# The RWKV stage of a five-block fp32 network: queues rearranged, and the squared keys for the norms in two fp32r parts

## The reference, cut to what matters

```python
def rwkv7_time_mix(x, mu, w_rkv, ...):
    xx = shift(x) - x                      # previous token minus this one
    xr, xw, xk, xv, xa, xg = (x + xx * mu[i] for i in range(6))
    r, k, v = xr @ w_r, xk @ w_k, xv @ w_v
    w = decay(tanh(xw @ w1) @ w2);  a = sigmoid(a0 + (xa @ a1) @ a2)
    g = sigmoid(xg @ g1) @ g2
    kk = normalise(k * k_k)                # per head of 64: divide by the root of the sum of squares
    k = k * (1 + (a - 1) * k_a)
    # per head, token by token: S = S*w + (S @ -kk) (kk*a)^T + v k^T ; y = S @ r
    return (group_norm(y) + bonus) * g @ w_o
```

## Time and profile before

| | us |
|---|---|
| median of 3 runs | 2152.41 (2149.99 to 2152.99) |
| the profiled execution | 2152.05 |
| its span in the trace | 2150.2 |
| busy in it: PE / DVE / ACT / POOL | 2005.9 / 871.6 / 928.4 / 923.5 |
| RWKV projections, first LoRA matmul to last V matmul | about 752.9 to 962.2 |

### The profile page before, as it was taken

The page is one execution under the profiler, slowest core; times in us unless marked ns, Lnnn a source line. Parts: engine busy times, 40 slices in busy tenths (PEclk is TensorE's granted clock), DMA queues, the critical chain, the costliest instruction groups (busy, mean ns, idle before and its releaser), DMA issues.

```text
span 2150.2 us, 32846 instructions
## 1 busy us (share of the span) xinstructions
PE 2005.9 (93%) x13218; PEld 1586.3 (74%) x13218; DVE 871.6 (41%) x1793; ACT 928.4 (43%) x1721; POOL 923.5 (43%) x641
## 2 busy tenths in 40 slices
PE   6999899999997899897888999999989999999998
PEld 5888566787765675676675888887877678888786
DVE  2103566310037494865654433331043733333301
ACT  3342677343256566532333544432153744344312
POOL 3332577244356434520127344445424634444542
PEclk9999999999998999996899999999999999999999
DMA  4323100233210222222102233333213022333322
GB/s 146 89 73 99 40 1 2 69 91 107 80 40 30 79 69 71 69 79 58 30 20 98 60 97 95 92 98 118 95 54 97 2 94 84 97 98 98 118 89 79
DMA packets 222376, 161.53 MB, mean 75 GB/s; under 512 B 28602, under 2 KB 205314, under 8 KB 222226
## 3 DMA queue, kind: packets, MB, share of 16 engines
q1 hardware_dynamic: 220034, 152.36, 23.9%
q0 software_dynamic: 2192, 7.07, 1.1%
HBM read 154.16 MB, written 5.24 MB: 74 GB/s over the span
## 4 chain that ended last, share of the span: by engine, by line
PE 78%; DVE 11%; ACT 3%; issue 3%; POOL 3%; DMA 1%; POOLq 1%; DVEq 0%; PEld 0%; PEldq 0%; SPq 0%; ACTq 0%
PE ps L389 15%; PE ps L351 13%; PE ps L353 13%; PE ps L362 13%; PE ps L399 7%; PE ps L1443 2%; PE ps L1456 2%; PE ps L1432 2%; DVE ps L970 1%; DVE buffer L3200 1%; POOL weights_lo L292 1%; DVE buffer L978 1%; DVE buffer L3202 1%; PE ps L2233 1%; PE ps L2255 1%
## 5 line engine op out<-in xcount | busy, mean ns | idle before, releaser
L292 POOL TENSOR_TENSOR weights_lo<-buffer,weights_hi 128x1024 fp32r<-128x1024 f32 (+1 forms) x266 | 659.4, 2481 | 901.1 <-ACT weights_hi L281 900.8
L281 ACT ACTIVATE weights_hi<-buffer 128x1024 fp32r<-128x1024 f32 (+1 forms) x266 | 277.9, 1048 | 298.9 <-PE ps L399 274.1
L351 PE MATMUL ps<-u_hi,weights_hi 128*128 128x512 f32 (+1 forms) x752 | 280.1, 380 | 5.6 <-DVE u_lo L706 3.0
L353 PE MATMUL ps<-u_lo,weights_hi 128*128 128x512 f32 (+1 forms) x736 | 279.6, 384 | 0.0
L2031 ACT ACTIVATE buffer<-ps,buffer 128x512 f32<-128x512 f32 x88 | 68.5, 778 | 282.9 <-PE ps L362 282.9
L2061 DVE SCALAR_TENSOR_TENSOR buffer<-ps,buffer,buffer 128x511 f32<-128x511 f32 x88 | 66.0, 750 | 294.2 <-ACT buffer L2031 294.2
L362 PE MATMUL ps<-u_hi,weights_lo 128*128 128x512 f32 (+1 forms) x752 | 176.6, 377 | 0.0
L351 PEld LDWEIGHTS ps<-u_hi,weights_hi 128*128 128x128 f32 x752 | 141.5, 190 | 33.1 <-issue 5.6
L353 PEld LDWEIGHTS ps<-u_lo,weights_hi 128*128 128x128 f32 x736 | 138.3, 188 | 30.0
L362 PEld LDWEIGHTS ps<-u_hi,weights_lo 128*128 128x128 f32 x752 | 136.5, 190 | 26.8 <-POOL weights_lo L292 0.2
L389 PE MATMUL ps<-weights_hi,act_hi 128*128 128x512 f32 x352 | 111.3, 397 | 0.5 <-issue 0.5
(11 more groups left out here) (431 smaller groups left out, 4117.4 us busy)
## 6 DMA issues: line engine op xcount, KB each, us to landing
buffer<-in_w_up SPq DMA_DIRECT2D x88, 512.0 KB, 3.8
buffer<-in_w_down SPq DMA_DIRECT2D x44, 512.0 KB, 3.3
buffer<-in_diff_w_in SPq DMA_DIRECT2D x32, 512.0 KB, 4.0
buffer<-in_nsa_w_in SPq DMA_DIRECT2D x28, 512.0 KB, 3.8
buffer<-in_w_rkv SPq DMA_DIRECT2D x24, 512.0 KB, 3.8
buffer<-in_nsa_w_out SPq DMA_DIRECT2D x8, 512.0 KB, 3.6
buffer<-in_diff_w_out SPq DMA_DIRECT2D x8, 512.0 KB, 3.7
buffer<-in_w_o_rwkv SPq DMA_DIRECT2D x8, 512.0 KB, 3.4
```

Source lines behind the costliest of these rows:

```text
L281: self.nc.scalar.activation(self.part_hi[:, part % self.PARTS, 0:n], self.raw[:, ld % self.RAW, 0:n], ACT.Copy).then_inc(self.hi_ready, 1)
L292: self.nc.gpsimd.tensor_tensor(self.part_lo[:, part % self.PARTS, 0:n], self.raw[:, ld % self.RAW, 0:n], self.part_hi[:, part % self.PARTS ...
L351: nc.tensor.matmul(out, hi[:, k, :], rhs[0][:, k, tokens], start=(k == 0), stop=False)
L353: nc.tensor.matmul(out, hi[:, k, :], rhs[1][:, k, tokens], start=False, stop=False)
```

## The change

1. **Norms.** The plain fp32 product of the squared keys becomes two fp32r products. DVE makes the raw square (`scalar_tensor_tensor` of K, k_k squared, K), ACT copies its high part, DVE subtracts for the low part, each in a single buffer. ACT's own square is gone. `squares(0)` and `squares(1)` both stand behind K2, and `squares(j-1)` behind Kj.
2. **Mix scratch** of the key and gate mixes moves from SBUF to PSUM banks 5 and 6. The mixes of V and R are made inside DVE's key loop, four for each j from 4 on.
3. **Second LoRA product** is interleaved with the gate products, so ACT's 16 sigmoids run beside them.
4. **Receptance loop.** `sums` 0 to 3 come before it, 4 to 7 in its first four rounds. `blocks` 0 to 3 stand behind R4 to R7; their upper halves are copied by DVE, in its own round.
5. **Values and core.** `blocks` 4 to 7 move from the core's list into the first V half. The blocks are stored piece by piece, the first four before the first slot of the second V half is fetched. The second inversion starts with the first item of the core's list.
6. **Transition.** The first half of the LoRA product comes after all four turns of x, with DVE's and ACT's items reordered.

The core of the diff (the loop with the mixes is DVE's, the one with `high` and `take` is ACT's):

```diff
         for j in range(2, KD):
             project_features(env, pe, self.k[j][0], m.mixes[self.K], self.k[j][1])
-            squares(j - 2)
+            if j == 2:
+                squares(0)
+            squares(j - 1)
...
+        for j in range(KD):
+            pair = (2 * j % KD, 2 * j % KD + 1)
+            for n in (self.G,) if j < 4 else (self.MIXED_V, self.MIXED_R):
+                for k in pair:
+                    mix(n, k)
+            if j < 4:
+                for k in pair:
+                    low(self.G, k)
+            if j:
+                square_low(j - 1)
+            square(j)
...
             high(n, k)
             high(n, k + 1)
+            if j:
+                square(j - 1)
             env.split_hi(act, ahead[j + 2])
             take(entry, m.k[:, j, :], ACT.Copy)
-            act.wait_ge(env.proj_taken, entry[1] + 1)
-            square(j)
...
         def blocks(n):
-            if n:
-                pe.wait_ge(self.core.blocks_taken, n)
-            else:
-                pe.wait_ge(self.shrink_taken, NT + 1)
+            pe.wait_ge(self.shrink_taken, NT if n < NT else KD)
+            if n:
+                pe.wait_ge(self.core.blocks_act, n)
+                pe.wait_ge(self.core.blocks_dve, n)
...
-            if k >= 5:
-                blocks(k - 5)
+            if k >= NT:
+                blocks(k - NT)
...
-            if k + 3 < KD:
-                sums(k + 3)
+            if k < NT:
+                sums(k + NT)
+            if k > NT:
+                take_blocks(k - 1 - NT)
             dve.wait_ge(env.proj_taken, g + 1)
             v.tensor_tensor(m.r[:, k, :], m.r[:, k, :], shrink, ALU.mult).then_inc(self.shrink_taken, 1)
...
-        self.order = [(name, 0) for name in first] + [("dg", n) for n in range(NT, 2 * NT)] + [(name, 1) for name in first]
+        self.order = [(name, n) for n in range(2) for name in first]
```

More of the change, by code:

```diff
@@ L2435, in __init__ @@
         self.blkX = env.take(BLK, BLK, at=slot(6))
-        self.diag = [env.take(32, BLK, at=slot(6)), second]
+        later = self.v[:, :, T:T + 256].rearrange("p n (u t) -> p n u t", t=BLK)
+        first = env.take(32, BLK, at=slot(6))
+        self.diag = [first[:, 8 * n:8 * n + 8, :] for n in range(NT)] + [later[:, n] for n in range(NT)]
         self.rk = [env.take(2, T, at=env.post_g_at), env.take(2, T, at=env.pair_at)]
@@ L2599, in tensor, with second @@
+            squares(j - 1)
         hid_hi, hid_lo = [h[:, 0, :] for h in m.hid]
         hi, lo = env.parts(self.second)
+        def second(k):
+            if k >= 2:
+                pe.wait_ge(env.proj_taken, self.second_group(k - 2, 1) + 1)
+            cols = slice(k * P, (k + 1) * P)
+            for w, x, first, last in ((hi, hid_hi, True, False), (hi, hid_lo, False, False), (lo, hid_hi, False, True)):
+                for which, rows in enumerate((slice(0, 64), slice(64, P))):
+                    done = mm(env.ps[:, 2 * (k % 2) + which, :], w[rows, 0, cols], x[rows, :], start=first, stop=last)
+                    if last:
+                        done.then_inc(env.proj_ready, 1)
@@ new lines, in gate_highs, with gate_lows @@
+        def gate_highs(n):
+            w, (x_hi, x_lo) = env.parts(self.g1[n])[0], m.mixes[self.G]
+            out = env.ps[0:w.shape[2], self.GATE + n, :]
+            env.wait_hi(pe, self.g1[n])
+            for k in range(KD):
+                if n == 0:
+                    mixed(self.G)(k)
+                mm(out, w[:, k, :], x_hi[:, k, :], start=(k == 0), stop=False)
+                mm(out, w[:, k, :], x_lo[:, k, :], start=False, stop=False)
+        def gate_lows(n):
+            w, x_hi = env.parts(self.g1[n])[1], m.mixes[self.G][0]
+            env.wait_lo(pe, self.g1[n])
+            for k in range(KD):
+                done = mm(env.ps[0:w.shape[2], self.GATE + n, :], w[:, k, :], x_hi[:, k, :], start=False, stop=(k == KD - 1))
+            done.then_inc(env.proj_ready, 1)
@@ L2603, in tensor @@
         pe.wait_ge(self.hid_ready, 2)
-        for k in range(KD):
-            g = self.second_g + 2 * k
-            env.wait_bank(pe, g)
-            env.wait_bank(pe, g + 1)
-            cols = slice(k * P, (k + 1) * P)
-            for w, x, first, last in ((hi, hid_hi, True, False), (hi, hid_lo, False, False), (lo, hid_hi, False, True)):
-                for which, rows in enumerate((slice(0, 64), slice(64, P))):
-                    done = mm(env.bank(g + which), w[rows, 0, cols], x[rows, :], start=first, stop=last)
-                    if last:
-                        done.then_inc(env.proj_ready, 1)
+        pe.wait_ge(env.proj_taken, self.k[-1][1] + 1)
+        second(0)
+        second(1)
+        gate_lows(0)
+        squares(KD - 1)
+        second(2)
+        second(3)
+        gate_highs(1)
+        second(4)
+        second(5)
+        gate_lows(1)
+        second(6)
+        second(7)
         def spread(k):
@@ new lines, in vector @@
+        step(v.tensor_tensor(m.k_k_squared, env.vec[:, V_B + 16:V_B + 24], env.vec[:, V_B + 16:V_B + 24], ALU.mult))
+        for k in range(KD):
+            mix(self.K, k)
+            if k:
+                low(self.K, k - 1)
+        dve.wait_ge(env.proj_ready, self.lora_g + 1)
+        low(self.K, KD - 1)
+        dve.wait_ge(self.hid_ready, 1)
+        v.tensor_tensor(m.hid[1][:, 0, :], m.hid_raw, m.hid[0][:, 0, :].bitcast(F32),
+                        ALU.subtract).then_inc(self.hid_ready, 1)
@@ L2728, in vector @@
         v.reciprocal(m.norms[0:48], m.norms[0:48]).then_inc(self.inv_ready, 1)
-        for k in range(3):
-            sums(k)
+        dve.wait_ge(env.proj_ready, self.gate_group(1) + 1)
+        for k in range(KD):
+            low(self.R, k)
         dve.wait_ge(self.norm_ready, 1)
@@ L2817, in scalar @@
         high(self.K, 7)
-        ahead = [ld for ld, _ in self.k] + [ld for ld, _ in self.g1] + [self.second] + [ld for ld, _ in self.r]
+        ahead = [ld for ld, _ in self.k] + [self.g1[0], self.second]
         for j, entry in enumerate(self.k):
@@ L3285, in vector @@
             op.then_inc(self.taken["D"], 1)
-            for _ in range(3 if key[1] < 2 and self.at[key] < self.at["S0", 0] else 2):
+            for _ in range(2):
                 next(running, None)
```

263 lines of the change are left out of this document (143 added, 120 removed).

## The result

The changed kernel takes 2155.47 (median of 20 runs) where the kernel before takes 2152.70 (20 runs beside them): a ratio of 1.0014, with a 95% interval of 1.0008 to 1.0021. One of the changed kernel's 20 runs took 4878.56, and the ratio leaves it out. The change is a loss, but a small one, within the 0.2% that were to count as no change; 2158.7 was forecast, and "slower by over 0.2%" was given more than half of the chances. The profiled execution has a span of 2153.0 for 2150.2: +2.8 where the sum said +6.7.

What follows compares the result with a forecast made beforehand. TensorE was taken to bound the kernel (78% of the chain, VectorE 11%). TensorE milestones ran -2.0, +8.6, +5.4, +13.6, +15.1, +9.2, +6.7, so 2152.05 + 6.7 = 2158.7; forecast's own range 2154 to 2164, rivals 2146 to 2167.

Steps and rivals of the forecast that it cites:

- slower by over 0.2%: Outcome class for the whole kernel: a time above 2156.7, given a chance of 0.52.
- K0 and K1: First two key groups: mix scratch in PSUM lets the low part start earlier, gain 1.9 (bounds 0 and 2.1).
- Key loop: K2 to the gate: TensorE waits for squares, 5.2 behind K2; the milestone moves from -2.0 to +8.6.
- the ring of three instructions: Key loop: the squares' DVE and ACT steps with POOL's split, period 6.8, then 8.2 from j = 4; PE needs 6.07.
- Rival (a): Key loop: raw square not held by POOL's split, gate starts at 824.3, total 2146.4, faster; chance 0.17.
- Gate to spread 0: Gate product to first spread: the path becomes DVE's, 28.4 in place of 31.6; milestone +5.4 (bounds +4 and +8).
- Receptance loop: Spread 0 to V: waits of 3.0 behind R5, R6 and R7, half clock after them, 67 for 58.9; milestone +13.6.
- Rival (b): Receptance loop: its gaps do not lower the clock, 61.5 for 67, total 2152, no change; chance 0.2.
- V and the core up to Z of piece 1: V +1.5 (0 to 2.5); then Z of piece 1 11.9 behind V's end in place of 17.8, -5.9; milestone +9.2.
- No gap before Z of piece 1: Core: a sign listed for the prediction, there worded as no gap before Z of piece 0.
- Core behind Z: After Z of piece 1: second inversion ends earlier, eight of 32 items already done, worth about 2.5 (1 to 5).
- ahead of the keys: Transition, span start to first key matmul: taken as 0, bounds -1 and +2.

Runs made afterwards that it cites:

- experiment 8: The kernel before, with only the scratch of the key and gate mixes moved to two PSUM banks; ratio 0.9987 to the kernel before.
- experiment 1: The changed kernel, with one operand of the raw square read from its PSUM bank in place of SBUF; ratio 1.0011 to the kernel before.
- experiment 2: The changed kernel, with the plain fp32 norm product as before the change, no raw square or low part on VectorE; ratio 0.9994 to the kernel before.
- experiment 6: The changed kernel, with VectorE's mixes for the next key group ahead of the raw square of this one; ratio 0.9988 to the kernel before.
- experiment 5: The changed kernel, with TensorE's norm product of group j behind key group j + 2 in place of j + 1; ratio 1.0026 to the kernel before.
- experiment 3: The changed kernel, with VectorE's copy of the blocks moved early in its receptance-loop round, right behind the end of the spread; ratio 0.9990 to the kernel before.
- experiment 4: The changed kernel, with the second inversion begun at the first state step, as before the change; ratio 1.0007 to the kernel before, median 2153.34.
- experiment 11: The changed kernel, raw square reading PSUM, mixes ahead of it, norm products (but the last) halfway through the group after next, blocks' copy early; ratio 0.9928, 2137.8.

## Why the prediction was near, and where it was off

The time came out at the low end of the forecast's range, and the class with the most chances, slower by over 0.2%, didn't come. The mechanisms named were the ones at work, but that the sum is within 3.9 is in part luck: 7.7 of errors one way stand against 3.8 the other way.

- **K0 and K1**: 1.9 forecast (2.0 in the milestones), 2.04 measured, and shown alone in experiment 8.
- **Key loop**: the mechanism was right (raw squares of 2.5; gaps of 4.6 behind K2 and 1.6 behind K5 to K7 for the 5 and 2 forecast, put down to DVE), the size was not: the ring of three instructions is 6.43 and 7.82, not 6.8 and 8.2, so +8.3 for +10.6. The sum took each instruction whole; in the trace GpSimd's split takes 2.4 for the 2.55 used, and one instruction starts before the one before it has ended. Over the loop this is 2.3. Experiments 1, 2 and 6 show that it is the ring: 1 and 6 shorten it, each in another way, and 2 takes it away; in experiment 5, where TensorE's place in it is another, its period stays. Rival (a), the raw square not held, is excluded as a forecast; made true in experiment 1, it moved the hold to the mixes and gave a third of what the rival said.
- **Gate to spread 0**: 28.4 forecast, 29.6 measured. The eight low parts behind the reciprocal took 6.99 as forecast, and TensorE waited twice for them (0.80 and 2.03 for R0). What was sized too small is TensorE's own part behind the last of them, the last high and the low products of R0: 2.4 forecast, 4.55 measured (856.03 to 860.58), at a granted clock of 0.65. The forecast had taken a gap of 2.12 to do no harm, by the earlier trace rows; here one of 2.03 was followed by slow matmuls. No run undoes the interleaving by itself, so the 1.9 gained in this stretch is read from the trace and not from an experiment.
- **Receptance loop**: 67 forecast, 65.1 measured. Three waits of 3.0 were forecast and three of 2.91 came; experiment 3 shows the cause. The wait in front of `blocks` 0 was 3.90 for 2.6, but ended where it was forecast to (29.3 behind the spread), since VectorE sets it. Half clock behind all of them was forecast and came behind some. Rival (b), no half clock, was wrong for the first two and right for the last two.
- **V and the core up to Z of piece 1**: from V's start to its end 48.8, +2.4 for +1.5; the half clock at its start, of which a part was expected to go, stayed (0.61 for 4.3). From V's end to Z of piece 1 13.6 for 17.8: -4.2 where -5.9 was forecast. "No gap before Z of piece 1" was wrong: it is 2.13, and 3.01 before that of piece 0. The steps of the second inversion were in the sum at 5.0 (eight of 0.5 and 1.0 for the memsets), and experiment 4 prices them at 5.2 over both pieces. So the 1.7 lies for the most part in what is left without them: 8.35 from V's end to Z of piece 1 in experiment 4, where the sum leaves 11.9 - 5.0 = 6.9. Which instruction was priced too low there stays open.
- **Core behind Z**: this is the term that was mis-sized most: 2.5 forecast, "worth about 2.5 (1 to 5)", 5.3 measured. Experiment 4 shows that the early start makes all of it: without it the last state step looked at lies 142.5 behind that Z, where it lay at 142.8 before; with it, at 137.4.

The terms that erred: 2.3 in the key loop, 1.9 in the receptance loop, 2.8 behind Z and 0.7 ahead of the keys made the time lower; 1.2 at the gate, 0.9 in V and 1.7 ahead of Z higher. That is 3.9, the difference between +6.7 and +2.8. Of the 0.7 ahead of the keys, nothing can be said: kernels that are alike up to there differ by more.

## What to carry to other kernels

Before a product is made cheaper, write down the ring of instructions that feeds it, engine by engine, and compare it with the period of the engine it is to help: here 0.52 a group was saved on TensorE by adding three instructions to a ring that was already at 4.8 of 6.6, and TensorE kept the gain as far as the gate only once the mixes stood ahead of the raw square and it took the product half a group later. Even then the next stretch, bound by other engines, gave it back (experiment 11). Ask of each copy that frees a bank where it stands in its engine's round: moving one copy of 1.2 within its round was worth 5.2, more than the 4.2 that the changed arithmetic could give at most. A gain that starts early on a shared engine (the second inversion) may be paid for by what it stands in front of.

## What the runs showed of the hardware

A gap of one length is not followed by one clock: of the waits of 2.91 in front of `blocks` 1 to 3, the first was followed by half clock and the other two not in the changed kernel, and all three in experiment 2 (0.68, 0.51 and 0.52), where the same instructions come 3 to 6 earlier. From one `blocks` to the next it takes 9.96 at full clock (913.40 to 923.36) and up to 12.8 (883.73 to 896.51 in experiment 2). In the changed kernel and in experiments 1, 4, 5 and 6 the three distances are 11.5 to 12.4, 11.3 to 11.5 and 9.95 to 9.96, so the pattern is not chance; in experiment 2 they are 12.8, 11.5 and 12.6. What decides stays open.

A DVE instruction with two SBUF inputs is held by GpSimd's split whether it writes to SBUF (the raw square) or to PSUM (the mixes of experiment 6, at 786.67 beside a split that began at 786.65):

```profile
786.67 3.60 DVE L2730 SCALAR_TENSOR_TENSOR ps<-buffer,buffer,buffer 128x512 f32<-128x512 f32 x2
```

It is 3.60 for two, where two that no split holds take 1.41. GpSimd is held as well when it comes second: its splits take 2.95 and 2.97 where a mix starts 0.03 and 0.04 before them (792.64 and 798.54 in experiment 6), and 2.40 where the split starts first (786.65).
